# Dummy products at four waits of TensorE, and GLA's two output tiles parted, in a two-block transformer kernel

## The reference

```
xn = x * rsqrt(mean(x * x) + 1e-6) * g            # mean over the 1024 channels: "the first sum"

# GLA, per head and chunk of 64
o_local = (causal(q_dec @ k_inv^T)) @ v
o_state = q_dec @ S ;  S = S * decay + k_end^T @ v

# RWKV-7, per head and chunk of 16: the state passes from chunk to chunk
S = M_c S + U_c ;  y = r S + ...

# HGRN-2, per head and chunk of 32
delta = (k * exp(b_last - b))^T @ v ;  S = decay * S + delta

# the router of the experts
logits = h @ w_router + b_router ;  top 4 of 32
```

## Time and profile before

| what | before |
|---|---|
| median of 3 runs | 2311.67 us |
| lowest and highest | 2309.2 and 2313.76 us |
| the profiled execution | 2312.33 us |
| its span in the trace | 2310.5 us |
| busy: PE, PE weight loads, DVE, ACT, POOL | 2155.1, 1426.8, 606.2, 370.4, 125.2 us |
| instructions in the trace | 25674 |

### The profile page before, as it was taken

One profiled execution on the slowest core, in us unless ns is written; L12 is line 12 of the kernel. 1 busy time (PEld: TensorE's weight loads), 2 busy tenths in 40 slices (PEclk: granted clock), 3 DMA queues, 4 the chain that ended last, 5 costly groups with the idle time before them and its releaser, 6 DMA issues.

```text
span 2310.5 us, 25674 instructions
## 1 busy us (share of the span) xinstructions
PE 2155.1 (93%) x10738; PEld 1426.8 (62%) x10738; DVE 606.2 (26%) x1209; ACT 370.4 (16%) x672; POOL 125.2 (5%) x186
## 2 busy tenths in 40 slices
PE   8999999999999999999999999996779999999764
PEld 6787878888878888888777854432323333433221
DVE  3344432233444313336224331000001010100001
ACT  3421112100005212000123231110000010001000
POOL 0023300000000000000000000010000000001000
PEclk9999999999999999999999999998889999999887
DMA  6221043333541535336533449999999999999995
GB/s 247 81 102 38 2 183 128 146 146 137 232 174 46 189 139 219 146 144 264 212 149 117 171 192 381 428 426 428 427 427 415 428 426 428 426 396 428 427 428 250
DMA packets 42572, 587.55 MB, mean 254 GB/s; under 512 B 5152, under 2 KB 5424, under 8 KB 6736
## 3 DMA queue, kind: packets, MB, share of 16 engines
q1 hardware_dynamic: 42448, 585.82, 62.2%
HBM read 584.75 MB, written 1.05 MB: 254 GB/s over the span
## 4 chain that ended last, share of the span: by engine, by line
PE 71%; DMA 25%; DVE 2%; ACT 1%; issue 1%; SPq 0%; PEld 0%; DVEq 0%; ACTq 0%; PEldq 0%
PE pb L409 70%; DMA ring<-in_gu 8%; DMA kv<-in_gu 7%; DMA ring<-in_dne 5%; DMA kv<-in_dne 3%; PE pb L419 1%; DMA arena<-in_gu 1%; DMA arena<-in_dne 1%; ACT arena L370 1%; DVE arena L326 1%; DMA arena<-in_dn 1%; DVE arena L311 0%; DMA col<-in_cols 0%; DVE ring L326 0%; DVE arena L320 0%
## 5 line engine op out<-in xcount | busy, mean ns | idle before, releaser
L409 PE MATMUL pb<-arena,ring 128*128 128x256 f32 (+3 forms) x2688 | 600.7, 382 | 5.8 <-DVE arena L326 3.6
L409 PE MATMUL pb<-arena 128*128 128x256 f32 (+12 forms) x2772 | 525.6, 385 | 40.3 <-DMA ring<-in_dne 26.0
L409 PEld LDWEIGHTS pb<-arena,ring 128*128 128x128 f32 (+3 forms) x2688 | 503.7, 189 | 95.2 <-issue 17.1
L409 PEld LDWEIGHTS pb<-arena 128*128 128x128 f32 (+5 forms) x2772 | 344.7, 170 | 209.7 <-issue 169.6
L409 PE MATMUL pb<-arena,cst 128*64 128x512 f32 (+6 forms) x1032 | 337.2, 619 | 63.4 <-DMA kv<-in_gu 41.0
L409 PE MATMUL pb<-ring,cst 128*64 128x512 f32 (+2 forms) x800 | 342.0, 629 | 0.0
L409 PEld LDWEIGHTS pb<-arena,cst 128*64 128x64 f32 (+4 forms) x1032 | 104.5, 141 | 268.8 <-issue 266.9
L409 PE MATMUL pb<-ring,arena 128*64 128x512 f32 (+2 forms) x480 | 195.2, 634 | 5.7 <-DMA arena<-in_dne 5.7
L376 ACT ACTIVATE arena<-pb 128x512 f32<-128x512 f32 (+4 forms) x123 | 68.8, 559 | 559.4 <-PE pb L419 423.9
L409 PEld LDWEIGHTS pb<-ring,cst 128*64 128x64 f32 (+2 forms) x800 | 100.0, 140 | 67.6 <-issue 67.6
L318 DVE TENSOR_SCALAR arena<-pb 128x512 f32<-128x512 f32 x30 | 20.8, 692 | 450.2 <-PE pb L409 450.2
(11 more groups left out here) (142 smaller groups left out, 1459.0 us busy)
## 6 DMA issues: line engine op xcount, KB each, us to landing
arena<-in_gu SPq DMA_DIRECT2D x60, 2048.0 KB, 18.3
ring<-in_gu SPq DMA_DIRECT2D x50, 2048.0 KB, 19.3
arena<-in_dne SPq DMA_DIRECT2D x36, 2048.0 KB, 19.3
ring<-in_dne SPq DMA_DIRECT2D x22, 2048.0 KB, 19.4
kv<-in_gu SPq DMA_DIRECT2D x18, 2048.0 KB, 19.4
ring<-in_up SPq DMA_DIRECT2D x13, 2048.0 KB, 7.6
ring<-in_ada SPq DMA_DIRECT2D x9, 2048.0 KB, 8.0
ring<-in_wkv SPq DMA_DIRECT2D x8, 2048.0 KB, 7.6
```

Of the source, the lines that this page charges most:

```text
L409: r = self.e.matmul(out, lhsT, rhs, start=start, stop=stop, skip_group_check=True)
```

## The change

Dummy products are added in five places: tile in0.w0 (10 products of 128 columns) ahead of the first sum and in0.w1 (13) behind it; rw.w (4 products of 256 columns) in the chunk pair c7 ahead of its tiles m and u; hg.w (2 of 256) between the transposes and the first state; and in the router three products of 256 columns into the unused half of tile mo.lg, behind chunks 1, 3 and 5. Nothing reads them. GLA's output tiles are parted: gla.o0 stays between the halves of the projection, gla.o1 goes behind the second half, and the fill of six steps moves ahead of gla.h0 and gla.h2. ACT's program is put into the same order.

```diff
         def mixer0_p(P):
             P.begin("in0")
             P.wait_ge("consts")
+            P.warm("in0.w0", ONESD, ONESD, 10)
             sum_p(P, "n0")
+            P.warm("in0.w1", ONESD, ONESD, 13)
             w = P.unit("ab_small")[:, 0:8 * 272].rearrange("p (k n) -> p k n", k=8)
...
-            def outputs():
-                for h2 in range(2):
-                    b = P.tile(f"gla.o{h2}")
-                    P.wait_ge("free gla.sc1", "free gla.st2")
...
+            def outputs(h2):
+                b = P.tile(f"gla.o{h2}")
+                P.wait_ge("free gla.sc1", "free gla.st2")
...
-            proj_p(P, "ab_r.2", "rkv.v", after_first=outputs)
+            proj_p(P, "ab_r.2", "rkv.v", after_first=lambda: outputs(0))
+            outputs(1)
             P.beside(kv_p(P, 0))
+            P.fill("rw.f0", FILLS[0])
             for j in (0, 2):
                 b = P.tile(f"gla.h{j}")
                 P.wait_ge(f"gla.sq{j}")
                 P.mm(b, ones, gsq[:, j:j + 2, :], True, True, sig=f"gla.h{j}")
-            P.fill("rw.f0", FILLS[0])
             heads("rw.b", "rw.rk", BE)
...
             for h2 in range(2):
+                if h2:
+                    rkv("v", 2)
                 b = S.tile(f"gla.o{h2}")
                 S.copy(go[:, h2:4:2, :], pair(b))
                 S.free(f"gla.o{h2}")
             for j in (0, 2):
                 S.act(gsq[:, j:j + 2, :], go[:, j:j + 2, :], ACT.Square)
                 S.mark(f"gla.sq{j}")
-            rkv("v", 2)
...
                 yield
                 yield
+                if n == "c7":
+                    P.warm("rw.w", ident, cst["tri"], 4)
                 b = P.tile(f"{n}.m")
                 b2 = P.tile(f"{n}.u")
...
             def first_states():
                 decayed()
+                P.warm("hg.w", ident, cst["tri"], 2)
                 state(0)
...
                          c == 7, sig="mo.lg" if (i == 1 and c == 7) else None)
+                if c in (1, 3, 5):
+                    P.mm(b[:, 256:512], ident, cst["tri"], False, False)
             back_p(P, XT, "mo.t")
```

More of the change, by code:

```diff
@@ L1061, in front_p @@
-            proj_p(P, "ab_r.2", "rkv.v", after_first=outputs)
+            def outputs(h2):
+                b = P.tile(f"gla.o{h2}")
+                P.wait_ge("free gla.sc1", "free gla.st2")
+                for q2 in range(2):
+                    hd = q2 * 2 + h2
+                    p0, j = 64 * (hd % 2), hd // 2
+                    for i in range(2):
+                        o0 = q2 * 256 + i * 128
+                        P.mm(b[:, o0:o0 + 128], gv[:, i, hd * 128:(hd + 1) * 128], gsc[:, hd % 2, j * 2 + i, :],
+                             True, False)
+                        for c in (2 * i, 2 * i + 1):
+                            if c == 0:
+                                continue
+                            end = q2 == 1 and c == 3
+                            P.mm(b[:, q2 * 256 + c * 64:q2 * 256 + c * 64 + 64], gst[p0:p0 + 64, j, c, :],
+                                 gq[p0:p0 + 64, j, c * 64:(c + 1) * 64], False, c % 2 == 1,
+                                 sig=f"gla.o{h2}" if end else None)
```

## The result

The median of six executions is 2320.55 us (2316.61 to 2323.86), against 2312.49 of six of the kernel before on the same chip: ratio 1.0038, 95% interval 1.0028 to 1.0049. Two later sets gave 1.0036 and 1.0033. The change makes the kernel 0.33 to 0.38% slower, some 8 us; I had forecast +2 (2313.7 us), with 2319.0 as the upper end of the range.

A forecast was written before the change was run, and what follows sets the result against it. PE was taken to bound the kernel until about 1,400 us, its gains reaching the end in full. Terms 5.7 - 4.6 - 1.65 + 4.5 - 1.9 = +2.05 on 2312.33 gave 2314.4, as median 2313.7 us; range 2306.5 to 2319.0.

The forecast's parts named there:

- The two waits: PE idle 8.6 us at gla.qk0 for a bank, and 3.7 us before the attention output's transposes at the first state.
- the five terms: Start +5.7, GLA -4.6, last chunk -1.65, first state +4.5 and router -1.9, summing to +2.05 us.
- Rival A: Router: the clock falls despite the dummies, +1.3 instead of -1.9, total 2316.9 us; chance 0.12.
- B: Start: dummy tiles cost nothing, no wait at gla.qk0; total 2302.3, or 2296.2 if the attention step stays too; chance 0.08.
- C: Start: 128-column dummies do not raise the clock before the sum, which costs 3.0 more, total 2316.7 us; chance 0.10.
- the start's -5.7: Start: gain from both sums and the projection at the full clock, -3.0 and -2.7 us, before the bank wait.
- GLA's -4.6: GLA output tiles and second projection half: 14.1 us at the full clock instead of 18.7; bounds -1.2 to -4.7.
- the last chunk's -1.65: Last chunk: dummies fill the 2.02 us wait for DVE, wide instructions end at 294.3 instead of about 296.0 us.
- the router's -1.9: Router: with the clock held, the ranks start at 1349.2 instead of 1351.07 us.
- A second step: Whole kernel: PE's gains or losses ahead of the expert loads carry to the end one for one.
- part 5: Router: dummy products after the first three pairs of chunks hold the clock, -1.9 us, up to +1.3 if it falls.
- The verdict "same" at 0.70: Whole kernel: no change beyond 0.2% (4.6 us), chance 0.70, against slower 0.19 and faster 0.11.

The follow-up runs named there:

- before_same: The kernel before, unchanged, timed and profiled a second time; ratio 0.9996 to the kernel before.
- p_start: The kernel before with only the two dummy tiles at the start, in banks 6 and 7, rotation untouched; ratio 0.9990.
- p_gla: The kernel before with only GLA's output tiles parted and the fill moved; ratio 0.9986.
- p_last: The kernel before with only the four dummy products in the chunk pair c7; ratio 1.0005.
- p_state: The kernel before with only the dummy tile hg.w, taken without advancing the attention stream; ratio 0.9997.
- p_router: The kernel before with only the three dummy products in the router's tile; ratio 0.9998.
- both1: The changed kernel with start tiles in banks 6 and 7 and hg.w not advancing the attention stream; 2302.77 us, ratio 0.9960 to the kernel before.
- both2: The changed kernel with start tiles in banks 6 and 7 and hg.w not advancing attention, timed again; 2305.25 us, ratio 0.9965 to the kernel before.
- start_few: The kernel before with the start's dummy tiles in banks 6 and 7, but 3 products behind the sum instead of 13; 2307.15 us, ratio 0.9984.

## Why the prediction was wrong, step by step

The same instructions were matched between traces and their starts subtracted. The table gives what a stretch costs against the first profile of the kernel before, the one that the sum was made with; the three profiles of the changed kernel are averaged, "same" is before_same, and "old code" are those among the single parts (in the order p_start, p_gla, p_last, p_state, p_router) that do not touch the stretch. The experts' row ends at PE's last instruction.

| stretch | forecast | changed, mean of 3 | same | old code |
|---|---|---|---|---|
| start, to 60 us | +5.7 | +5.1 | -0.7 | -2.2, -2.7, -2.1, -1.1 |
| GLA, 60 to 160 | -4.6 | -4.6 | -1.3 | -1.3, -1.3, 0, -1.3 |
| last chunk, 160 to 296 | -1.65 | -1.7 | -1.7 | -1.7, 0, 0, -1.7 |
| wait at 607 | 0 | +1.1 | 0 | 0, 0, 0, 0 |
| 700 to 760 | 0 | +0.5 | 0 | +1.7, 0, +1.7, 0, +1.7 |
| first state, 1240 to 1280 | +4.5 | +4.2 | -1.6 | 0, -1.6, 0, 0 |
| router, 1340 to 1353 | -1.9 | -1.7 | -1.7 | 0, -1.65, -1.6, -1.6 |
| narrow products, 1385 to 1395 | 0 | +1.6 | +1.6 | 0, +1.6, +1.6, +1.6, +1.6 |
| experts, from 1395 | 0 | +1.5 | +0.9 | +2.6, +1.2, +3.5, +3.8, +3.3 |

**Right.** The two waits, place, cause and size: 8.78 us of idleness where I had 8.6, resumed at 37.31 (36.9), and PE standing 3.6 us (3.7) before the transposes. Only the price of the low clock behind the first wait was too high, 1.6 us where I had 2.6. Against the first profile, GLA, the last chunk and the router came out within 0.2 us of their terms, and the five terms together are +1.3 where I had +2.05. Rival A is out (no fall in the router in any of the eight profiles with its dummies), B is out by the waits, C by the sum's 3.72 us. On the wait for a bank I had set the code against a rule of the Trainium skill ("Perfetto Trace Analysis", Optimization Strategy), that repeating gaps on the engine can mean a shortage of PSUM. The old trace has no such gaps, and still two tile calls too many cost 10.6 us. The page does not state the converse that rival B made of it, and the runs refute that: the absence of gaps does not show that a bank is free for the next tile.

**The step that failed** is the size of the gains in the sum: the start's -5.7 that the wait was set against, GLA's -4.6, the last chunk's -1.65 and the router's -1.9. The sum was made against one execution, and I took its falls of the clock for the code's. That profile had a fall at each of the five places; its time was typical only because it had fewer in the experts (every other profile but one loses 0.3 to 3.8 us more there). So the gains were read as full where the old code pays them in part of its executions. Counted over all sixteen profiles, the old code has a low clock in GLA in 7 of 7 and in the router in 8 of 8, but behind the last chunk's wait in 5 of 8 and at the first state in 5 of 7, and where it has one its length differs (in the router 6.8 us in three, 3.4 in five). With the first profile counted as 0, the start of the old code is on average 1.5 us shorter over its six profiles in the table, GLA's stretch 0.9, the last chunk's 0.85, the first state's 0.5 and the router's 1.1, and a change can save only what is left: 3.8 of the start's 5.3 (less the 1.0 at 607, where p_start has 2.3), 3.7 of GLA's 4.6, 0.85 of the last chunk's 1.7 and 0.6 of the router's 1.7. I had bounded the terms' sizes, but as errors of mine about a fixed event, not as an event that may be absent.

Taken against the mean of the old code's profiles in each row of the table, the five places cost the changed kernel +6.1 us, where the forecast has +2.05, and all other stretches together +0.6. The same count fits both1 and both2: their profiles gain 14.4 and 15.0 us at the five places against the first profile, and some 10 against the mean, of which 1.0 goes at 607.

**A second step failed too**, by less: "what PE gains or loses ahead of them I carry to the end one for one". Against the first profile the stretches outside the five places, which I had at zero, come to +4.7: the transfer at 607 (1.1, shown by start_few), the narrow products at 1385 (1.6), a fall at 730 us in one of the three profiles (0.5) and the experts (1.5). But the old code's profiles have the last three as well, 1.1, 0.7 and 2.2 us on average, so only the 1.1 at 607 is a loss that the change itself makes, besides what follows the router. There part 5 is undone: in every one of the profiles in which the router keeps its clock or has it low for 3.4 us only, changed or not, the clock is low for 6.8 us behind about 1380 and 1.6 us are lost; in the three in which the router had its full fall (the first profile of before, p_start, start_few) it is low for 3.4. The router's -1.9 is worth -0.1, and alone it measured nothing.

This accounts for some 6.7 of the 8 us between the medians. The rest stays open; a few profiles of a kernel give its mean to about 1 us at best, and two of the changed kernel's three, at 2316.6 and 2316.2, were the shortest of their sets. Which fall comes in which execution is not settled, nor why 700 to 760 us has a fall in about half of all profiles.

The verdict "same" at 0.70 was too sure in any case: a sum of -15.5 and +17.5 us, in which each piece is uncertain by one or two, cannot be known to 4.6 us with that confidence.

## What to carry to other kernels

A helper that takes a tile does more than its products: look what else the call advances, here the bank rotation (10.6 us) and a side stream (3 to 6 us), and give a dummy a bank of its own and no step. Before counting on a dummy to save a fall of the clock, read several profiles of the unchanged kernel; a fall that stands in one may be absent in the next, and one that is avoided can come at the next narrow stretch. Count a dummy's instructions too: 46 more of them moved an instruction fetch into a transfer on the path (1.0 us).

## What the runs showed of the hardware

Equal idle times left the clock down in one execution and up in another: 2.02 and 0.97 us in two of the same program, 2.97 us in two kernels with the same start. One instruction packet of 16 KB inside a weight transfer of 2 MB went with 1.0 us more for that transfer; the packet's own bytes are under 1% of the transfer's, so it delays more than its size. In the new trace the packet itself takes 6.3% of the 16 DMA engines' time from 603 to 604 us, 1.0 us on one engine, which is as much as the transfer is late; that it holds one engine for that time, and the transfer with it, is an estimate and was not tried. The smaller packet of q14 lies in the transfer in both traces and makes no difference. How often a fall came with and without dummies, over sixteen profiles: in the router in 0 of 8 with and 8 of 8 without, at the last chunk in 0 of 8 and 5 of 8, at the first state in 0 of 5 (with the attention step in place) and 5 of 7, in GLA in 2 of 9 with the tiles parted and 7 of 7 before.
